# Moving all memory K/V projection tiles of a hybrid decoder step into a new first stage

## What is computed

```
h = rms_norm(x, norm_mix_g[0])                       # x: 1024 + 8 tokens, 1024 wide
sb_q, sb_k, sb_v, sb_z, qkv, g_z, g_a, g_b = split(h @ w_in)
k_all = concat([past_k, k_rows]);  v_all = concat([past_v, v_rows])     # samples: 4096 paged past rows each
o_sb = stick_breaking(sb_q, k_all, v_all, bias, pos) * silu(sb_z)
...
mem_k[l], mem_v[l] = mem_prompt @ xa_wk[l], mem_prompt @ xa_wv[l]       # 256 memory tokens, l = 0, 1
```

## Time and profile before

| | |
|---|---|
| median of 3 runs | 3474.35 us (3473.98 to 3491.3) |
| profiled execution, first to last instruction | 3474.9 us |
| PE busy | 2970.1 us (85%) |
| DVE / ACT / POOL busy | 1611.0 (46%) / 845.2 (24%) / 538.6 us (16%) |
| DMA, mean over the span | 141 GB/s |

### The profile page before, as it was taken

One profiled execution on the slowest core, in us unless ns is written; L12 is line 12 of the kernel. 1 busy time (PEld: TensorE's weight loads), 2 busy tenths in 40 slices (PEclk: granted clock), 3 DMA queues, 4 the chain that ended last, 5 costly groups with the idle time before them and its releaser, 6 DMA issues. The chain is left out here.

```text
span 3474.9 us, 47776 instructions
## 1 busy us (share of the span) xinstructions
PE 2970.1 (85%) x17599; PEld 2575.6 (74%) x17599; DVE 1611.0 (46%) x2091; ACT 845.2 (24%) x1310; POOL 538.6 (16%) x537
## 2 busy tenths in 40 slices
PE   5888887979997688878888899999998888889787
PEld 5867776754443678778757899999887778889557
DVE  4577767626666567334142422111166643241423
ACT  2111111127765210122122200011122332121231
POOL 0022222213222122110001011000033301110011
PEclk9989998879998899889999999999988988999898
DMA  2678989763103200231363222222255553212641
GB/s 108 231 277 312 328 308 324 270 220 97 43 13 117 76 19 18 80 119 49 134 218 110 73 103 94 88 97 95 84 184 178 203 178 122 88 37 75 239 159 62
DMA packets 234222, 489.08 MB, mean 141 GB/s; under 512 B 38153, under 2 KB 99210, under 8 KB 233746
## 3 DMA queue, kind: packets, MB, share of 16 engines
q1 hardware_dynamic: 202514, 391.29, 33.0%
q0 software_dynamic: 22800, 76.64, 6.3%
q10 hardware_dynamic: 8784, 19.52, 1.5%
HBM read 378.84 MB, written 112.78 MB: 141 GB/s over the span
## 5 line engine op out<-in xcount | busy, mean ns | idle before, releaser
L413 PE MATMUL ps<-in_hi,w_hi 128*128 128x344 f32 x2592 | 837.2, 323 | 101.0 <-DVE in_lo L316 101.0
L414 PE MATMUL ps<-in_lo,w_hi 128*128 128x344 f32 x2592 | 834.1, 322 | 0.0
L415 PE MATMUL ps<-in_hi,w_lo 128*128 128x344 f32 x2592 | 833.4, 322 | 0.0
L413 PEld LDWEIGHTS ps<-in_hi,w_hi 128*128 128x128 f32 x2592 | 492.6, 190 | 105.7 <-DVE in_lo L316 105.7
L414 PEld LDWEIGHTS ps<-in_lo,w_hi 128*128 128x128 f32 x2592 | 492.5, 190 | 0.0
L415 PEld LDWEIGHTS ps<-in_hi,w_lo 128*128 128x128 f32 x2592 | 492.5, 190 | 0.0
L1238 PE MATMUL ps<-in_hi,wv_hi 128*128 128x344 f32 (+1 forms) x952 | 307.6, 323 | 4.7 <-DVE wv_lo L1056 4.0
L1239 PE MATMUL ps<-in_lo,wv_hi 128*128 128x344 f32 (+1 forms) x952 | 300.9, 316 | 0.0
L1240 PE MATMUL ps<-in_hi,wv_lo 128*128 128x344 f32 (+1 forms) x952 | 300.4, 316 | 0.0
L272 DVE CAST w_hi<-w_raw 128x1024 fp32r<-128x1024 f32 x68 | 50.6, 744 | 535.0 <-PE ps L415 502.4
L276 POOL TENSOR_TENSOR w_lo<-w_raw,w_hi 128x1024 fp32r<-128x1024 f32 x40 | 95.3, 2389 | 1016.0 <-ACT w_hi L272 1016.0
(11 more groups left out here) (317 smaller groups left out, 4625.3 us busy)
## 6 DMA issues: line engine op xcount, KB each, us to landing
k_pages<-in_cache_k SPq DMA_DIRECT2D x256, 256.0 KB, 4.7
v_pages<-in_cache_v POOLq DMA_DIRECT2D x256, 256.0 KB, 5.0
cc<-stage SPq DMA_DIRECT2D x48, 516.0 KB, 2.7
w_raw<-in_w_c SPq DMA_DIRECT2D x48, 512.0 KB, 4.3
in_raw<-og SPq DMA_DIRECT2D x40, 516.0 KB, 5.7
wv_raw<-in_w_mem SPq DMA_DIRECT2D x32, 512.0 KB, 7.4
xs_kv<-in_mem_k SPq DMA_DIRECT2D x16, 1024.0 KB, 7.1
xs_kv<-in_mem_v SPq DMA_DIRECT2D x16, 1024.0 KB, 5.7
```

The costliest lines, as they stand in the source:

```text
L413: pe.matmul(o, w_hi[:, u, a:b], h, start=(kt == 0), stop=False)
L414: pe.matmul(o, w_hi[:, u, a:b], l, start=False, stop=False)
L415: return pe.matmul(o, w_lo[:, u, a:b], h, start=False, stop=(kt == KT - 1))
```

## The change

The block of `linear` with `fresh` and the block of `load_split` are replaced by one block, `head`. Its list of tiles is 24 memory tiles, the 4 Q tiles, 8 memory tiles. The norm chain of x runs beside the memory tiles: a square with each of tiles 2 to 9, an addition with 3 to 10, the partition sums on PE after tile 12, the inverse root at 13, and scaling and splitting of one k-tile of x with each of tiles 14 to 21. Weights go through three raw buffers and three split buffers. In `weave` the memory tiles are gone: each step has three tiles, at j = 0, 3 and 6, and the raw weight buffers are three instead of two. The outputs are the same.

```diff
+HEAD_ORDER = tuple(("mem", n) for n in range(24)) + tuple(("q", n) for n in range(HEAD_Q)) + tuple(
+    ("mem", n) for n in range(24, HEAD_MEM))
+def head(k, x_t, mem_t, tables, w_ab, w_mem, gains, g_col, hi, lo, ab, mem_kv):
+    RAW, W, ST = 3, 3, 2
+    SUMS_AT, NORM_AT = 12, 14
...
+            def weights(n):                                  # SP
+                if n >= RAW:
+                    sp.wait_ge(lo_done, n - RAW + 1)
+                sp.dma_start(raw[:, n % RAW, :], w_mem[t] if kind == "mem" else w_ab[AB_Q + t]).then_inc(loaded[n % RAW], 16)
...
+            sp.dma_start(mem[:, :, :], mem_t.rearrange("t p n -> p t n")).then_inc(mem_in, 16)
+            for n in range(RAW):
+                weights(n)
+            for kt in range(KT):
+                sp.dma_start(x[:, kt, :], x_t[kt]).then_inc(x_in[kt], 16)
+                if kt == 0:
+                    for dst, src in tables:
+                        sp.dma_start(dst, src).then_inc(tables_in, 16)
+            for n in range(N):
+                if n + RAW < N:
+                    weights(n + RAW)
+                if n >= 1:
+                    store(n - 1)
...
+            for n in range(N):                               # ACT
+                if n + 2 < N:
+                    high(n + 2)
+                if 2 <= n < 2 + KT:
+                    square(n - 2)
+                if n == NORM_AT - 1:
+                    inverse_root_mean(act, k, rstd, ps[:, SUM_BANK:SUM_BANK + NCH, 0:CH], sum_done, log_done, r_done)
+                if NORM_AT <= n < NORM_AT + KT:
+                    kt = n - NORM_AT
+                    act.wait_ge(y_done, kt + 1)
+                    act.copy(hi[:, kt, :], y[:, kt % 2, :]).then_inc(x_hi_done, 1)
+                evacuate(n)
...
+            for n in range(N):                               # DVE
+                if n + 2 < N:
+                    low(n + 2)
+                if 3 <= n < 3 + KT:
+                    ... sumsq += sq
+                if NORM_AT <= n < NORM_AT + KT:
+                    kt = n - NORM_AT
+                    if kt + 1 < KT:
+                        scaled(kt + 1)
+                    low_input(kt)
...
-W_ORDER = (("plain", 0, 0), ("mem", 0, 1), ("plain", 1, 2), ("mem", 1, 0), ("silu", 0, 1), ("mem", 2, 2),
-           ("mem", 3, 1))
+W_ORDER = (("plain", 0, 0), ("plain", 1, 1), ("silu", 0, 2))
+W_AT = (0, 3, 6)
-    A_BANK, M_BANK, SUMB, OB, CB = 0, 3, 5, 6, 7
+    BANK = (0, 3, 0)
+    SUMB, OB, CB = 6, 7, 6
+    COL = W
-        raw = sb("wv_raw", [128, 2, KT * 128])
+        raw = sb("wv_raw", [128, 3, KT * 128])
...
                 for j in range(NJ):                          # SP, DVE and PE alike
-                    if j < NPOS:
-                        tile(s, first, j)
+                    if j in W_AT:
+                        tile(s, first, W_AT.index(j))
                     values(s, j, first)
...
-            load_split(k, ins["mem_t"], 0, m_hi, m_lo, MEM)
```

More of the change, by code:

```diff
@@ L492, in _ @@
                 sp.wait_ge(stored[u], 16 * (KT // SLOTS))
[L495 to L525, removed]
 SB_STEPS = [(u, c, i) for u in range(2) for c in range(2) for i in range(4 * c + 3, -1, -1)]
@@ L916, in weave @@
+W_PLAIN, W_SILU = 2, 1
+W_ORDER = (("plain", 0, 0), ("plain", 1, 1), ("silu", 0, 2))
+W_AT = (0, 3, 6)
+def weave(k, early0, w_ab, hi, lo, ab, og, cache_k, cache_v, page_table, bias):
     k.recycle(0)
@@ L929, in sem @@
             return k.semaphore(k.name(name))
-        raw = sb("wv_raw", [128, 2, KT * 128])
+        raw = sb("wv_raw", [128, 3, KT * 128])
         w_hi, w_lo = sb("wv_hi", [128, 3, KT * 128], f32r), sb("wv_lo", [128, 3, KT * 128], f32r)
         stage = sb("wv_stage", [128, 3, NT])
-        m_stage = sb("wv_mem_stage", [128, 2, MEM])
         pt = sb("page_table", [1, S * NP], mybir.dt.int32)
@@ L948, in weave @@
         hi_done, lo_done, mm_done, evac_done = sem("w_hi"), sem("w_lo"), sem("mm"), sem("evac")
-        stored = [sem(f"w_stored{n}") for n in range(5)]
+        stored = [sem(f"w_stored{n}") for n in range(3)]
         (setup, q_rows, q_copied, prod_done, red_done, zb_done, zc_done, e_done, l_done, sp_done, suf_done,
@@ L955, in weave @@
         NE = AB_V - early0
-        early_in = [sem(f"early_in{n}") for n in range(2)]
+        early_in = [sem(f"early_in{n}") for n in range(3)]
         early_stored = [sem(f"early_st{n}") for n in range(3)]
@@ L960, in weave @@
         block = ctx.enter_context(nc.Block())
-        RAW = [pos % 2 for pos in range(NPOS)]
         SLOT = [x[2] for x in W_ORDER]
-        BANK = [M_BANK + n % 2 if kind == "mem" else A_BANK for kind, n, _ in W_ORDER]
         def back(of, pos):
@@ L971, in store_slot @@
         def store_slot(kind, n):
-            return {"plain": n, "silu": 2, "mem": 3 + n % 2}[kind]
+            return {"plain": n, "silu": 2}[kind]
         def at(step, first, pos, d):
@@ L1005, in weights @@
                 kind, n, _ = W_ORDER[pos]
-                v = at(s, first, pos, back(RAW, pos))
+                v = at(s, first, pos, back(SLOT, pos))
                 if v is not None:
@@ L1010, in weights @@
                     sp.wait_ge(early_lo, NE)
-                t = {"plain": AB_V + W_PLAIN * s + n, "silu": AB_Z + s, "mem": W_MEM * s + n}[kind]
-                sp.dma_start(raw[:, RAW[pos], :], dram_tile(w_mem if kind == "mem" else w_ab, t)).then_inc(loaded[pos], 16)
+                t = {"plain": AB_V + W_PLAIN * s + n, "silu": AB_Z + s}[kind]
+                sp.dma_start(raw[:, SLOT[pos], :], dram_tile(w_ab, t)).then_inc(loaded[pos], 16)
             def k_pages(s, j, first):
@@ L1020, in step @@
                 for j in range(NJ):
-                    if j < NPOS:
-                        weights(s, first, j)
+                    if j in W_AT:
+                        weights(s, first, W_AT.index(j))
                     if not last:
@@ L1027, in _ @@
                 if j < NE:
-                    if j >= 2:
-                        sp.wait_ge(early_lo, j - 1)
-                    sp.dma_start(raw[:, j % 2, :], w_ab[early0 + j]).then_inc(early_in[j % 2], 16)
+                    if j >= 3:
+                        sp.wait_ge(early_lo, j - 2)
+                    sp.dma_start(raw[:, j % 3, :], w_ab[early0 + j]).then_inc(early_in[j % 3], 16)
                 k_pages(0, j, True)
@@ L1053, in split @@
                     dve.wait_ge(early_mm, NE)
-                dve.tensor_copy(w_hi[:, slot, :], raw[:, RAW[pos], :]).then_inc(hi_done, 1)
+                dve.tensor_copy(w_hi[:, slot, :], raw[:, slot, :]).then_inc(hi_done, 1)
                 dve.wait_ge(hi_done, NPOS * s + pos + 1)
-                dve.tensor_tensor(w_lo[:, slot, :], raw[:, RAW[pos], :], w_hi[:, slot, :].bitcast(f32),
+                dve.tensor_tensor(w_lo[:, slot, :], raw[:, slot, :], w_hi[:, slot, :].bitcast(f32),
                                   ALU.subtract).then_inc(lo_done, 1)
@@ L1105, in early_split @@
             def early_split(n):
-                dve.wait_ge(early_in[n % 2], 16 * (n // 2 + 1))
+                dve.wait_ge(early_in[n % 3], 16 * (n // 3 + 1))
                 if n >= 3:
                     dve.wait_ge(early_mm, n - 2)
-                dve.tensor_copy(w_hi[:, n % 3, :], raw[:, n % 2, :]).then_inc(early_hi, 1)
+                dve.tensor_copy(w_hi[:, n % 3, :], raw[:, n % 3, :]).then_inc(early_hi, 1)
                 dve.wait_ge(early_hi, n + 1)
-                dve.tensor_tensor(w_lo[:, n % 3, :], raw[:, n % 2, :], w_hi[:, n % 3, :].bitcast(f32),
+                dve.tensor_tensor(w_lo[:, n % 3, :], raw[:, n % 3, :], w_hi[:, n % 3, :].bitcast(f32),
                                   ALU.subtract).then_inc(early_lo, 1)
@@ L1126, in step @@
                 for j in range(NJ):
-                    if j < NPOS:
-                        split(s, first, j)
+                    if j in W_AT:
+                        split(s, first, W_AT.index(j))
                     if not last:
@@ L1161, in column @@
                 act.wait_ge(col_done, s + 1)
-                act.copy(osT[:, :, bass.ds(s, 1)], ps[:, CB, 0:4].rearrange("p (f o) -> p f o", o=1)).then_inc(os_done, 1)
+                act.copy(osT[:, :, bass.ds(s, 1)], ps[:, CB, COL:COL + 4].rearrange("p (f o) -> p f o", o=1)).then_inc(os_done, 1)
             def evacuate(s, first, pos):
@@ L1170, in evacuate @@
                         act.wait_ge(early_stored[e], 16 * len(range(e, NE, 3)))
[L1171 to L1184, removed]
+                if not first:
+                    act.wait_ge(stored[st], 16 * s)
+                act.activation(stage[:, st, :].rearrange("p (c n) -> p c n", c=NCH), ps[:, BANK[pos]:BANK[pos] + 3, 0:CH],
+                               AF.Silu if kind == "silu" else AF.Copy).then_inc(evac_done, 1)
+                act.wait_ge(evac_done, NPOS * s + pos + 1)
+                t = AB_Z + s if kind == "silu" else AB_V + W_PLAIN * s + n
+                act.dma_start(dram_tile(ab, t), stage[:, st, :]).then_inc(stored[st], 16)
```

(16 more changed lines are left out.)

130 lines of the change are left out of this document (128 added, 2 removed).

## The result

The changed kernel is slower: median 3615.07 us (3602.37 to 3620.69, 4 runs) against 3482.82 (3473.98 to 3493.74, 4 runs), ratio 1.0372 with a 95% interval of 1.0346 to 1.0398. The profiled execution spans 3600.7 us against 3474.9, 125.8 more. I had said 3595 from a sum of 3596 for the profiled execution.

The account below looks back on a forecast made before the run. No engine is full in a step; a ring of waits bounds it, with period 78.7 us instead of 71.1 forecast. 3474.9 + 65 (start) + 53 (seven steps) + 3 (last step) = 3596, stated as 3595 us, range 3540 to 3630.

Parts of the forecast that it names:

- The start, +65: Before weave: 32 added memory tiles against removed idle stretches; weave begins at about 169 us instead of 104, bounds +54 and +75.
- The lead-in, 0: Start of weave, before the eight steps: stays PE-bound with its five x tiles, so no change.
- The two waits for V: In each step PE idles for V pages over 7 us before values(2) and values(5), none before 6 and 7.
- Group 2: V group asked for only after values(0): 1.07 + 1.32 + 4.27 + 6.1 us with K loading, so values(2) starts at 29.3.
- Group 5: V group after values(3): 1.32 + 4.27 + 3.8 us, K not being loaded, so values(5) runs from 54.6 to 56.5.
- The clock: After each V wait PE restarts at granted clock 0.50: values 1.93 us instead of 1.07, tiles 1 and 2 12.9 instead of 11.4.
- ACT's order: End of each step: softplus queues behind tile 2's evacuation, so 9.3 us pass from the tile's end to the next t.
- DVE waiting for it some 20 us: Profile sign in each step: ACT's Exp right after the silu evacuation, with DVE waiting some 20 us for it.
- The last step, +3: Final step of weave, without K loads or softplus: 68.9 us against 66.
- Rival 1: Steps keep their length: pages land faster, clock recovers within values; period 69.7 to 73, total about 3540; chance 13%.
- rival 3: Slower than forecast: head starves PE, clock falls there too, or V lands at 6.9; +75 and 83.8, 3640; chance 12%.
- Rival 2: Faster: V loads don't hold PE, steps shrink to 55 us, total 3418; decides once a period is under 63; chance 3%.

Follow-up runs that it names:

- e1: The kernel before with the new head in place of its first block, so memory tiles are computed twice: 3553.80 us, 1.0189 of the kernel before, period 71.03.
- e2: The changed kernel with four buffers for V groups instead of two: 3460.21 us, 0.9911 of the kernel before, period 61.13.
- e3: The changed kernel with PE's tiles at j = 2, 4, 6 (weights and splits at 0, 3, 5): 3457.03 us, 0.9903 of the kernel before, period 61.08.
- e6: The changed kernel without K page loads of groups 2 to 7 (sample outputs differ): 3586.24 us, 1.0307 of the kernel before, period 77.75.
- e5: The changed kernel with 54 extra matmuls ahead of values(2) and of values(5) in each step: 3577.18 us, 1.0276 of the kernel before, period 76.1.
- e4: The changed kernel with softplus(s + 1) ahead of the step's last evacuation on ACT: 3549.95 us, 1.0187 of the kernel before, period 72.35.
- e8: The changed kernel with tiles at 2, 4, 6 and softplus ahead of the last evacuation: 3474.20 us, 0.9955 of the kernel before, period 61.05.
- e9: The changed kernel with four V buffers, tiles at 2, 4, 6 and softplus first: 3450.45 us, 0.9880 of the kernel before, period 59.09.

## Why the prediction was right, step by step

- **The start, +65.** Measured +62.2. The queue order did what I read from it (fourth weight tile at 25.6 for 24.9, tile 3 at 28.0 for 27.2), the last memory tile ended at 162.5 for 165.1. Too large was the memory tile: back to back they come every 2.88 us (evacuations from 142.45 to 162.60, seven intervals), and I had taken the 2.98 of a tile among `values`. The bounds of 54 and 75 held.
- **The lead-in, 0.** Measured -0.4.
- **The two waits for V.** The largest claim, that a stage loses time by losing work, holds: e1 gives the work back and the period with it, and e2 and e3 take most of the wait away in two ways (from 157.1 us of PE's time to 17.4 and 41.0), and with it 18.6 and 18.7 us a step. Group 2 was priced nearly right, by two misses that offset each other: it lands 5.2 us after its last issue and not 6.1, but that issue comes 6.2 us after the release and not 5.6. Group 5 lands 5.3 us after its last issue and not 3.8. The premise that no K is being loaded then was wrong: groups 0 and 1 of a later sample's K are still coming. SP's queue issues eight of those pages from 442.3 to 451.1, V group 5 is issued from 447.8 to 452.0, the DMA share in that wait is 0.94, and e6 has 3.2 us for a group without K beside it and 5.5 for one with. This is the term that was sized too small: 1.4 us a step.
- **The clock.** 13.3 and 13.4 us for tiles 1 and 2 instead of 12.9; e5 shows that the price is real, 3.65 us of the step there, and part of it was still paid in e5.
- **ACT's order.** 9.56 for 9.3, and e4 takes it away. My sign "DVE waiting for it some 20 us" was too low by my own sum (z at t + 46, Ln done at t + 74.6): it waited 28.6. The gain doesn't add to that of the V waits: on top of e3 it is worth nothing (e8), and on top of e2 it and the tiles' new places together 2.0 us (e9).
- **The last step, +3.** The match with +3.4 is luck: the step itself grew by 0.5 us, not 3, and the other 2.9 lie behind weave, where I had put nothing.
- **Sum.** 62.2 - 0.4 + 60.6 + 3.4 = 125.8, against 65 + 53 + 3 = 121: 2.8 too much at the start against 7.6 too little in the steps. The median over all runs lies 20 us above the number; 5.7 of these are the profiled execution's 3600.7 against 3595, and the other 14.4 come from the median being above the profiled execution (3615.07), as that of the kernel before is by 7.9 (3482.82 against 3474.9).
- **The rivals.** Rival 1 (steps of 69.7 to 73) did not happen: the two landings that PE waited for took 5.2 and 5.3 us, not the 2.8 of the lower rows, and the tiles behind them 13.3 and 13.4. Nor did rival 3: the head cost 62.2 and not 75, and its granted clock was 0.98. Rival 2 set its point at a period of 63, and e2, e3, e8 and e9 are on its far side and below the kernel before, by 0.45 to 1.2%; what I had called the floor of 69.7 is the floor for tiles at 0, 3 and 6 with two buffers only. My own figure of 55 for steps without a V wait was 4 to 6 too low each time: I had left the K pages out, for which DVE waits 55.9 to 68.7 us in all in these four runs, against 31.5 in the changed kernel.

The change itself, then, is half good: the memory tiles fill the idle start (32 tiles of 2.88 us, 92 us of PE, lengthen it by 62), and the whole loss and more comes from where the three remaining tiles were put.

## What to carry to other kernels

A filler job between two steps of a double-buffered stream is not idle work to be cleared away: count how long a buffer takes from its release to its next landing (here 1.4 us to the first issue, 4.2 to 4.8 to the fourth, and 5.2 to land), and keep that much other work between every two consumers, or more buffers. When work is moved out of a loop, place anew what remains: position alone was worth 18.7 us a step here (e3). And look at every in-order queue for what now stands behind a later item, as ACT's softplus did.

## What of the hardware was not expected

In e5 the granted clock fell to 0.50 for some 3 us, at 452 us, with PE busy. Before that PE had worked for 23 us, paused for 2.15, and worked again for over a microsecond; the pause before was 1.97 us. In the kernel before, a pause of 2.31 us left `values(6)` at 1.06 us. What makes the difference can't be told from these runs.
